# Turning v once into a DRAM copy and loading it chunk by chunk in a chunked RWKV recurrence, with other engine orders

## The reference, cut to what matters

```python
def wkv_scan(s0, r, w, k, v, a, b, reverse):
    def step(s, inp):
        r_t, w_t, k_t, v_t, a_t, b_t = inp
        sa = jnp.einsum('bhvk,bhk->bhv', s, a_t)
        s = s * w_t[:, :, None, :] + sa[..., :, None] * b_t[:, :, None, :] + v_t[..., :, None] * k_t[:, :, None, :]
        return s, jnp.einsum('bhvk,bhk->bhv', s, r_t)
    xs = tuple(jnp.moveaxis(z, 1, 0) for z in (r, w, k, v, a, b))
    s, y = lax.scan(step, s0, xs, reverse=reverse)
    return jnp.moveaxis(y, 0, 1), s
```

## Time and profile before

| | us |
|---|---|
| median of 3 runs | 2601.62 |
| lowest and highest of them | 2598.08, 2608.76 |
| the profiled execution | 2604.29 |
| its span | 2602.5 |
| its preparation stage (rwkv_prepare) | 1280 to 1372 in the span |
| its recurrence (rwkv_chunks) | 1372 to 1779 in the span |

### The profile page before, as it was taken

The page is one execution under the profiler, slowest core; times in us unless marked ns, Lnnn a source line. Parts: engine busy times, 40 slices in busy tenths (PEclk is TensorE's granted clock), DMA queues, the critical chain, the costliest instruction groups (busy, mean ns, idle before and its releaser), DMA issues. The chain is left out here.

```text
span 2602.5 us, 50127 instructions
## 1 busy us (share of the span) xinstructions
PE 2314.5 (89%) x20892; PEld 1847.3 (71%) x20892; DVE 1688.6 (65%) x2155; ACT 1025.3 (39%) x1633; POOL 661.3 (25%) x659
## 2 busy tenths in 40 slices
PE   5998988899999669999777999999973999999993
PEld 2886755568877558888636899997652888888883
DVE  5990559551115445666576776774657999999994
ACT  3112541231014420001154545444132877777773
POOL 1331568123320023222006666650000100000000
PEclk8998999999999779999878999998986999999997
DMA  6232004421104445211053111104142999999994
GB/s 237 96 124 75 1 33 142 132 99 45 49 14 185 151 156 193 96 41 40 14 185 92 32 32 29 29 20 169 57 174 97 409 407 396 396 393 405 396 378 158
DMA packets 136485, 401.77 MB, mean 154 GB/s; under 512 B 56314, under 2 KB 67834, under 8 KB 108754
## 3 DMA queue, kind: packets, MB, share of 16 engines
q1 hardware_dynamic: 124180, 360.02, 37.3%
q0 software_dynamic: 4608, 16.78, 2.7%
q10 hardware_dynamic: 7488, 21.99, 2.2%
HBM read 341.05 MB, written 57.69 MB: 153 GB/s over the span
## 5 line engine op out<-in xcount | busy, mean ns | idle before, releaser
L3900 DVE TENSOR_TENSOR ex_wl<-ew_raw,ex_wh 128x2048 fp32r<-128x2048 f32 x192 | 435.6, 2290 | 41.7 <-ACT ex_wh L3862 38.2
L3862 ACT ACTIVATE ex_wh<-ew_raw 128x2048 fp32r<-128x2048 f32 x192 | 367.6, 1919 | 109.5 <-PE ex_U L3806 40.3
L118 PE MATMUL sp_acc<-b2h_hi,sp_wh 128*128 128x512 f32 (+1 forms) x528 | 194.7, 369 | 16.2 <-POOL sp_wl L1729 16.2
L118 PE MATMUL sp_acc<-b2h_lo,sp_wh 128*128 128x512 f32 (+1 forms) x528 | 194.4, 368 | 0.0
L118 PE MATMUL sp_acc<-b2h_hi,sp_wl 128*128 128x512 f32 (+1 forms) x528 | 194.2, 368 | 0.0
L3783 POOL DMA_INDIRECT x<-ex_o,ex_at x16 | 26.5, 1656 | 490.2 <-DVE ex_o L3923 490.2
L2621 PE MATMUL rc_chain<-rc_x,rc_near 64*64 64x64 f32 x3200 | 132.8, 222 | 5.3 <-DVE rc_near L2503 2.2
L1727 POOL CAST sp_wh<-sp_w 128x1024 fp32r<-128x1024 f32 x26 | 28.3, 1088 | 402.2 <-DMA sp_w<-in_w_conv 221.4
L2621 PEld LDWEIGHTS rc_chain<-rc_x,rc_near 64*64 64x64 f32 x3200 | 111.1, 135 | 19.2 <-issue 9.0
L118 PEld LDWEIGHTS sp_acc<-b2h_hi,sp_wh 128*128 128x128 f32 x528 | 100.1, 190 | 33.9 <-POOL sp_wl L1729 16.6
L118 PEld LDWEIGHTS sp_acc<-b2h_lo,sp_wh 128*128 128x128 f32 x528 | 100.2, 190 | 16.4
(11 more groups left out here) (520 smaller groups left out, 5887.6 us busy)
## 6 DMA issues: line engine op xcount, KB each, us to landing
ew_raw<-in_exp_gate SPq DMA_DIRECT2D x64, 1024.0 KB, 8.0
ew_raw<-in_exp_up SPq DMA_DIRECT2D x64, 1024.0 KB, 9.5
ew_raw<-in_exp_down SPq DMA_DIRECT2D x64, 1024.0 KB, 8.0
b2p_pT<-in_ada_w SPq DMA_DIRECT2D x32, 512.0 KB, 6.0
rc_ac<-ac SPq DMA_DIRECT2D x40, 256.0 KB, 3.4
b_pj<-in_ada_w SPq DMA_DIRECT2D x8, 1024.0 KB, 12.5
ssm_wm<-in_w_merge SPq DMA_DIRECT2D x16, 512.0 KB
ac<-rp_ac SPq DMA_DIRECT2D x4, 2048.0 KB, 7.1
```

Source lines behind the costliest of these rows:

```text
L118: ins = nc.tensor.matmul(out, w[a][:, k, :], h[b][:, k, cols], start=(first and n == 0), stop=(last and n == 2))
L3862: nc.scalar.activation(wh[:, n % RING], raw[:, n % RING], ACT.Copy).then_inc(q["w_hi"], 1)
L3900: V.tensor_tensor(wl[:, n % RING], raw[:, n % RING], wh[:, n % RING].bitcast(f32), ALU.subtract).then_inc(q["w_lo"], 1)
```

## The change

Three things.

1. `rwkv_prepare` gets a DRAM tensor `v_dram` (1280 rows of tokens, 512 columns). Ahead of everything else PE turns v, ten tiles of 128 tokens with four 128x128 transposes each, into the six banks of `acc`; ACT copies each tile to `v_staged` (the space of `wide`), behind Tanh and behind the wait for `rates_in`; SP stores it. The first `logits` now waits for all ten copies, `widened(0)` for all ten stores.
2. `rwkv_chunks` loses `v_staged` on POOL, `v_rows` on PE and on ACT. In their place SP issues, per chunk, eight DMAs of 64 partitions with 2 x 256 bytes each (`load_v`). They wait for `state` and `outputs` of the chunk before, as the copies of ACT did. `load_v(0)` stands ahead of `ahead`, the others behind `load(c + 2)`. `right_side` waits for `v_loaded`.
3. The lists of POOL, ACT, DVE and PE are new. POOL's, ACT's and DVE's show the same steps in other places, and `weigh` stays at the end of DVE's loop body.

```diff
             def _(pe):
+                for i in range(TILES):
+                    if i >= 6:
+                        pe.wait_ge(q["v_out"], i - 5)
+                    for b in range(HP):
+                        last = nc.tensor.transpose(acc[:, i % 6 // 2, i % 2, b * P:(b + 1) * P], pT[:, VB + b, i * P:(i + 1) * P], T.ident[:])
+                    last.then_inc(q["v_turned"], 1)
...
                     if u == 0:
+                        pe.wait_ge(q["v_out"], TILES)
                         pe.wait_ge(q["lora_in"], 16)
...
                 act.wait_ge(q["rates_in"], 32)
+                for i in range(TILES):
+                    act.wait_ge(q["v_turned"], i + 1)
+                    nc.scalar.activation(v_staged[:, i], acc[:, i % 6 // 2, i % 2], ACT.Copy).then_inc(q["v_out"], 1)
...
+                def load_v(c):
+                    for d in range(2):
+                        if c:
+                            sp.wait_ge(joint["s_done"], c)
+                        if c > CTX_CK:
+                            sp.wait_ge(joint["y_crossed"], c - CTX_CK)
+                        for e in range(2):
+                            own = t[d]["uv"][e * CK:(e + 1) * CK].rearrange("p f (j a) t -> p f j a t", a=2)
+                            rows = v_dram[at(c, d):at(c, d) + CK, :].rearrange("r (j a f t) -> r f j a t", a=2, f=2, t=CK)
+                            for f in range(2):
+                                sp.dma_start(own[:, f, :, 1 - e, :], rows[:, f, :, 1 - e, :]).then_inc(q[d]["v_loaded"], 16)
...
                 def right_side(c):
                     if runs(c):
                         each("near_ready", 2 * c + 2)
-                        each("v_rows", 2 * c + 2)
+                        each("v_loaded", 64 * (c + 1))
...
                 for k in range(NCK + 2):
-                    lower(k - 1, 1)
-                    inverted(k - 2)
...
                     key_rows(k, 0)
                     chained_x(k - 1, 0, 4)
                     right_side(k - 1)
                     chained_x(k - 1, 1, 4)
                     lower(k, 0)
-                    right_side_of_state(k - 1)
+                    lower(k, 1)
+                    inverted(k - 1)
+                    key_rows(k, 1)
+                    solved(k - 1)
+                    chained_x(k, 0, 0)
+                    chained_x(k, 1, 0)
```

More of the change, by code:

```diff
@@ L2120, in _, with rwkv_chunks @@
                         products(n + 2)
-def rwkv_chunks(nc, T, I, pT, nkk, ac_dram, y, ahead, weigh):
+def rwkv_chunks(nc, T, I, pT, nkk, ac_dram, v_dram, y, ahead, weigh):
     LEVELS = 5
@@ L2150, in rwkv_chunks @@
                 b[n] = ph.sb(f"{n}{d}", [P, HP, CK])
[L2151 removed]
+            for n in ("e_neg", "tmp", "t1", "g", "sum", "S"):
                 b[n] = ph.sb(f"{n}{d}", [P, HP, CK])
@@ L2447, in _ @@
+                    kept(k - 1, 0)
+                    key_rows(k - 1, 0, 0)
+                    right_side(k - 2, 0)
+                    key_rows(k - 1, 1, 0)
+                    right_side(k - 2, 1)
+                    decay_out(k, 1)
+                    inverse(k - 2, 0)
+                    inverse(k - 2, 1)
+                    filled(k, 1)
+                    decay_in(k, 1)
+                    decay_in(k, 0)
+                    solved(k - 2, 0, 0)
                     factored(k - 1, 0, 0)
-                    inverse(k - 2, 1)
@@ L2449, in _ @@
-                    decay_in(k, 0)
+                    solved(k - 2, 1, 0)
                     factored(k - 1, 1, 0)
@@ L2571, in _ @@
                     dve.sem_inc(q[d]["y_added"], 1)
-                for k in range(NCK + 1):
+                for k in range(NCK + 2):
+                    advanced(k - 2, 0, 3)
+                    advanced(k - 2, 1, 3)
+                    turned(k - 2, 0, 4)
+                    last_factor(k - 2, 0)
+                    turned(k - 2, 1, 4)
+                    last_factor(k - 2, 1)
+                    right_side(k - 2, 0)
+                    right_side(k - 2, 1)
+                    masked(k - 1, 0)
+                    masked(k - 1, 1)
+                    turned(k - 1, 0, 0)
+                    turned(k - 1, 1, 0)
+                    outputs_of_state(k - 2, 0)
+                    outputs_of_state(k - 2, 1)
+                    advanced(k - 1, 0, 0)
+                    advanced(k - 1, 1, 0)
+                    turned(k - 1, 0, 1)
+                    outputs(k - 2, 0)
+                    outputs(k - 2, 1)
+                    turned(k - 1, 1, 1)
+                    summed(k - 2, 1)
+                    advanced(k - 1, 0, 1)
+                    advanced(k - 1, 1, 1)
+                    summed(k - 2, 0)
+                    turned(k - 1, 0, 2)
+                    turned(k - 1, 1, 2)
@@ L2770, in _ @@
                 for k in range(NCK + 2):
-                    lower(k - 1, 1)
-                    inverted(k - 2)
-                    chained_x(k - 1, 0, 0)
-                    key_rows(k - 1, 1)
-                    chained_x(k - 1, 1, 0)
+                    outputs_of_state(k - 2)
                     advanced(k - 1, 0, 0)
-                    solved(k - 2)
                     advanced(k - 1, 1, 0)
+                    outputs(k - 2)
                     chained_x(k - 1, 0, 1)
-                    outputs_of_state(k - 2)
                     chained_x(k - 1, 1, 1)
+                    state(k - 2)
                     advanced(k - 1, 0, 1)
-                    outputs(k - 2)
                     advanced(k - 1, 1, 1)
```

146 lines of the change are left out of this document (45 added, 101 removed).

## The result

| | median, us | runs, us | against before |
|---|---|---|---|
| before | 2600.39 | 2597.32 to 2608.76 | |
| after | 2620.29 | 2609.46 to 2622.95 | ratio 1.0067, 95% interval 1.0044 to 1.0091 |

The account below looks back on a forecast made before the run. PE was taken to set the recurrence's pace, 19.61 us a chunk. Recurrence -10, loads of v 0 and preparation +5 sum to -5, so 2601.6 - 5 = 2597 us, range 2582 to 2615.

Parts of the forecast that it names:

- The loads of v: Recurrence, SP: all eight landed 5.6 us after `state` ends, `right_side` needs them at 7.8; nothing waits, 0 us.
- the rows of v come late: Rival, recurrence: v's loads land late, from 4.2 us on; 2616 at 5.2, 2644 at 6.7; chance 0.08.
- The orders: Recurrence: 1.44 us a chunk goes, 0.89 comes back, 19.61 to 19.06; -10 us, bounds -29 and +9.
- The waits that come back: Recurrence, PE: waits of 0.30 behind `state`, 0.30 behind `firsts` and 0.29 before `solved`; 0.89 us a chunk.
- The rival that the state comes late: Rival, recurrence: POOL or DVE misses the state's 2 us margin by 1, so +1 a chunk, 2617; chance 0.10.
- fetches that fall badly: Recurrence: 2 us for instruction fetches, counted only in the +9 upper bound.
- The preparation: Preparation: first `logits` 6.7 us later, the clock gives 2 back; +5 for the stage, bounds +3 and +7.
- -2 by the clock: Preparation: transposes raise the clock to 2.4 GHz, speeding first `logits` and part of first squares; 1 to 3 us, taken -2.
- The rival on the clock: Rival, preparation: clock stays up through the squares, -12 in the stage; with the recurrence -17, 2585; chance 0.10.
- The sum: Whole kernel: -10 recurrence, 0 loads of v, +5 preparation make -5 us, so a median of 2597.

Follow-up runs that it names:

- x5: Changed kernel with v laid out for four loads a chunk of 64 KB in 64 pieces of 1 KB, not eight of 32 KB; measured time not in the text given.
- x1: Changed kernel without the loads of v for all chunks but the first (later chunks compute with wrong v): 2600.78 us, ratio 0.9998.
- x10: x5 with ACT's wait for restart (`rates_in`) moved behind the ten copies of v in the preparation: 2596.07 us, ratio 0.9996.
- x11: x5 with the turning of v moved from the preparation's start to its units 16 to 20, two tiles a unit: 2599.89 us, ratio 1.0007.
- x4: Kernel before with the changed preparation alone; v is turned, copied and stored but nobody reads it: 2607.40 us, ratio 1.0024.
- x8: x1 with every load of ac from chunk 2 on issued a second time into a spare tile: 2604.95 us, ratio 1.0022.
- x9: x1 with eight unread loads a chunk of 4 KB, 16 pieces of 256 bytes, where v's loads stood: 2601.22 us, ratio 1.0010.
- x2: Changed kernel with SP's loads reordered: v then ac of one direction, then v and ac of the other: 2674.88 us, ratio 1.0272.
- x6: As x5, four loads a chunk of 64 KB, but each in 256 pieces of 256 bytes; measured time not in the text given.
- x7: Changed kernel with x5's layout but eight loads a chunk of 32 KB in 64 pieces of 512 bytes; 11 us faster than the changed kernel by medians.

## Why the prediction was wrong

- **The loads of v: the step that failed.** I had 0.2 + 3.4 + 2.0 = 5.6 us to the last landing, 7.8 to need, nothing waits. The need was right: in x5 the first issue lies 7.8 ahead of an undisturbed `right_side`. So was the release (0.18, forecast 0.2). Both other terms were too small, and one was missing. The issues took 0.65 from start to start and not 0.49, and in most chunks one or two of the eight took 1.0 to 1.9: 5.3 to 6.8 from the first issue to the end of the last. Landing took 2.0 to 3.6, and PE started 0.27 behind the last landing, for which I had nothing. So the last of a chunk's loads landed 6.9 to 8.9 behind the first issue and not 5.4. The decision point of my rival, a landing of 4.2, was worked out with issues of 0.49; at 5.3 to 6.8 for eight, the last begins 4.7 to 6.2 behind the first, and a landing of 2.8 down to 1.3 decides. The long issues tip it in most chunks: eight of the usual length, 7 x 0.65, with the median landing of 2.5 and the 0.27 come to an estimate of 7.3, still inside 7.8 (the one chunk without a long issue waited 0.79 all the same, for a landing of 3.6). So the rival "the rows of v come late" was the case, 0.5 a chunk on average and not 1 to 2.5, and my 0.08 for it was far too low. The rows by which I had priced issue and landing came from another stage; why an issue is shorter there, with as many pieces, stays open.
- **The orders.** -10 for the recurrence, measured without v -5.0 (361.6 against 366.6). The clean chunk was 19.18 where I had 19.06: 0.43 less than before, and not 0.55. The waits that come back are as counted (0.31 + 0.29 + 0.29 in x1, 0.89 as forecast), so 1.32 went and not 1.44. But I took the clean chunk for all: 2.8 us more of stops inside groups than before, and an end that was 1.7 slower (the last interval 17.9, before 16.2), took most of the rest. The -5.0 is of two profiles and carries their scatter: the same orders gave 362.9 to 366.4 in x5, x10 and x11, the orders of before 371.4 in x4. The rival that the state comes late was not the case: in the changed kernel POOL had scaled the state 1.4 to 2.5 us before PE read it (forecast 2).
- **Stops inside groups.** I had 2 us for "fetches that fall badly" in the upper bound only. In the changed kernel they are 9.3, before 1.7. Of the 23, 19 end 1.2 to 1.5 us behind the end of a DMA of 16 KB on the queue that the view calls instruction (the others 1.9 to 2.4), and such a DMA starts every 4.4 us on average. I take the blocks for PE's: there are 87 in the recurrence, and PE ran 21541 matmuls and weight loads in it, the other three engines 1466 instructions together. The Trainium skill (Runtime: NRT & Kernel Launch, Instruction fetch mechanics) has it that PE's sequencer fetches the next 16 KB block on a DMA queue of its own while it executes, and that the cost is mostly hidden. For the kernel before the trace agrees, 1.7 of 366.6 us; for the changed kernel it was 9.3 of 378.6, and why is not shown. How much of the 4.8 between x1 and the changed kernel comes from v's pieces stays open; x8 and x9 bound it by a few us.
- **The preparation.** Forecast +6.7 for the first `logits`, -2 by the clock, +5 in all. Measured 6.3, and 4.3 to 4.4 at the stage's end. Right, by the steps that were given. 24 transposes took 0.22 each at a granted clock of 0.52, and the following 16 took 0.13 at 0.99. The rule that I had weighed (the Trainium skill, TensorE: Matmul & The Clock Gate, Part 4: PE-mode transpose: the full clock doesn't engage for transposes) doesn't hold in this trace either. The rival on the clock counted the -2 twice: 6.7 - 12 - 10 = -15, so 2586 and not 2585.
- **The sum.** Forecast -5; the terms measured are +3 preparation, -5 orders, +17 loads of v, +3 scatter of the profile: 18.

## What to carry to other kernels

A load's time to need is the whole chain: the wait that releases the queue, every issue ahead of it, and the landing of the last. With many small loads on one queue the issues are the largest term, at 0.6 us each for 16 to 64 KB here, so cut their number first (a layout in which one load's part lies together) and the size of pieces second. Leave room for an issue that takes 1.9, and for 0.3 from the last landing to PE's start; and never let a load that must wait for a buffer stand ahead of one that is urgent. A wait is paid again where the clock falls behind it: in x2 a wait of 3 us a chunk made the next groups 1.5 us longer. A new order has to be judged with its transfers: the same orders were worth -5 without the loads and +12 with them.

## What was not expected of the hardware

**An issue on SP that begins beside an instruction fetch of PE often lasts until the fetch has landed.** From the records of SP and of the DMA packets, loads of v and ac (and of x9's small ones) in the 19 chunks:

```
          issues   median us   over 0.85 us   of these: start -0.25 to +0.45 us from a fetch's start
before      32       0.52            0                0
after      184       0.60           30               30
x5         108       0.59           16               14
x6         108       0.60           15               14
x7         184       0.60           32               32
x9         184       0.42           23               21
```

All 30 long issues of the changed kernel, 0.93 to 1.88 us, begin within half a microsecond of the start of a 16 KB fetch and end 0.31 to 0.47 us behind its landing. It is so for loads of 4 KB (18 of the 23 in x9) as for some of 256 KB (3 of the 30). But six other issues of the changed kernel began in such a window and were short, 13 in x9 and all five in the kernel before; what else it takes I didn't find.

**"issue" in the view of waits can be a DMA.** All waits for v at `right_side` were listed so; the tile's own view and the records of the loads showed what they were. The Trainium skill (DMA: Bandwidth & Descriptors, Issuing engines are not separate DMA queues) says that initiating DMAs on several engines saves only the issuing sequencer's time, which is usually small relative to the DMA itself. For one load this trace agrees, 0.60 to issue and 2.5 to landing; for eight behind one another the issues took 5.3 to 6.8 us while the landings overlapped, so that time was the larger part.
